# Latent attention: the probabilities' multiplication by the inverse of their sum moved from VectorE to GpSimd

## The reference

```python
def block(args):
    ql, qr = args
    s = (jnp.einsum('bqhc,bkc->bhqk', ql, c_kv)
         + jnp.einsum('bqhr,bkr->bhqk', qr, k_rope))
    p = jax.nn.softmax(s.astype(jnp.float32), axis=-1).astype(c_kv.dtype)
    return jnp.einsum('bhqk,bkc->bqhc', p, c_kv)
```

## Time and profile before

| | before |
|---|---|
| median of 3 runs | 3429.01 us (3424.55 to 3431.45) |
| the profiled execution, whole | 3426.68 us |
| its span, first to last instruction | 3425.0 us |
| PE busy | 3135.5 us, 92% |
| DVE busy | 1681.2 us, 49% |
| ACT busy | 1171.0 us, 34% |
| POOL busy | 620.6 us, 18% |
| granted TensorE clock, mean | 0.947 of full speed |

### The profile page before, as it was taken

One profiled execution on the slowest core, in us unless ns is written; L12 is line 12 of the kernel. 1 busy time (PEld: TensorE's weight loads), 2 busy tenths in 40 slices (PEclk: granted clock), 3 DMA queues, 4 the chain that ended last, 5 costly groups with the idle time before them and its releaser, 6 DMA issues.

```text
span 3425.0 us, 39752 instructions
## 1 busy us (share of the span) xinstructions
PE 3135.5 (92%) x13884; PEld 2458.6 (72%) x13884; DVE 1681.2 (49%) x2588; ACT 1171.0 (34%) x2027; POOL 620.6 (18%) x363
## 2 busy tenths in 40 slices
PE   5999969999899997588899998997999999979999
PEld 3888846888588885376588876775777767767777
DVE  5554576554553335785411113474566324745653
ACT  3222233222232323364322223534444335344442
POOL 0000000000000001001244443124211331242113
PEclk8999979999999999799899999898899998989999
DMA  4655513554343232101222332112111220121112
GB/s 187 196 176 167 176 44 123 185 176 161 115 154 117 86 110 69 28 13 35 68 87 97 98 98 75 31 56 81 56 43 44 80 74 25 56 87 56 43 39 80
DMA packets 88731, 316.03 MB, mean 92 GB/s; under 512 B 10272, under 2 KB 11168, under 8 KB 88480
## 3 DMA queue, kind: packets, MB, share of 16 engines
q1 hardware_dynamic: 65424, 235.69, 21.6%
q0 software_dynamic: 19488, 71.31, 6.2%
q10 hardware_dynamic: 3696, 7.38, 0.7%
HBM read 310.14 MB, written 2.10 MB: 91 GB/s over the span
## 4 chain that ended last, share of the span: by engine, by line
PE 43%; issue 42%; POOL 10%; DVE 3%; DMA 1%; ACT 1%; POOLq 0%; SPq 0%; DVEq 0%; ACTq 0%
PE psum L365 36%; POOL w_lo L350 10%; PE psum L1886 3%; PE psum L881 1%; PE psum L558 1%; DVE rstd L441 1%; PE psum L851 1%; DMA ada_first<-ada_in 1%; DVE ada_acc L544 1%; PE psum L1830 0%; DVE X L521 0%; DVE ta L515 0%; DVE tb L477 0%; DMA raw<-stream_in 0%; PE psum L1832 0%
## 5 line engine op out<-in xcount | busy, mean ns | idle before, releaser
L350 POOL TENSOR_TENSOR w_lo<-raw,w_hi 128x1024 fp32r<-128x1024 f32 x229 | 551.0, 2413 | 1814.8 <-ACT w_hi L321 1619.6
L365 PE MATMUL psum<-h_hi,w_hi 128*128 128x512 f32 x1856 | 501.7, 404 | 44.5 <-DVE h_lo L489 31.6
L365 PE MATMUL psum<-h_hi,w_lo 128*128 128x512 f32 x1856 | 491.9, 398 | 0.0
L365 PE MATMUL psum<-h_lo,w_hi 128*128 128x512 f32 x1856 | 491.5, 398 | 0.0
L365 PEld LDWEIGHTS psum<-h_hi,w_hi 128*128 128x128 f32 x1856 | 353.2, 191 | 138.3 <-issue 55.1
L365 PEld LDWEIGHTS psum<-h_hi,w_lo 128*128 128x128 f32 x1856 | 352.4, 190 | 85.1
L365 PEld LDWEIGHTS psum<-h_lo,w_hi 128*128 128x128 f32 x1856 | 351.9, 190 | 85.6
L335 ACT ACTIVATE w_hi<-raw 128x1024 fp32r<-128x1024 f32 x256 | 257.1, 1046 | 142.3 <-DMA raw<-stream_in 138.4
L341 DVE TENSOR_TENSOR w_lo<-raw,w_hi 128x1024 fp32r<-128x1024 f32 x192 | 227.8, 1222 | 105.1 <-ACT w_hi L335 98.5
L688 DVE TENSOR_TENSOR tb<-ta,psum 128x512 f32<-128x512 f32 x88 | 60.3, 685 | 404.0 <-PE psum L365 359.8
L642 ACT ACTIVATE a_hi<-tb 128x512 f32 (+1 forms) x88 | 55.6, 632 | 554.4 <-DVE tb L688 554.4
(11 more groups left out here) (371 smaller groups left out, 4692.0 us busy)
## 6 DMA issues: line engine op xcount, KB each, us to landing
raw<-stream_in SPq DMA_DIRECT2D x437, 512.0 KB, 3.5
ada_raw<-ada_in POOLq DMA_DIRECT2D x128, 512.0 KB, 4.6
ada_first<-ada_in POOLq DMA_DIRECT2D x2, 2048.0 KB, 21.1
ada_first<-ada_in SPq DMA_DIRECT2D x2, 2048.0 KB, 24.3
X<-xT_in ACTq DMA_DIRECT2D x1, 2048.0 KB, 8.9
out_x<-X SPq DMA_DIRECT2D x8, 256.0 KB, 2.0
qt_hi<-qr_hi ACTq DMA_DIRECT2D x16, 64.0 KB, 2.0
qt_lo<-qr_lo ACTq DMA_DIRECT2D x16, 64.0 KB, 2.0
```

The lines of the kernel that those rows point to most:

```text
L350: pool.tensor_tensor(w_lo[:, u % RING], raw[:, u % RAW], w_hi[:, u % RING].bitcast(F32), ALU.subtract).then_inc(lo_ready, 1)
L365: mm = pe.matmul(dst, w[wi], m[mi], start=(first and n == 0), stop=(last and n == total - 1), skip_group_check=skip)
```

## The change

In the latent attention alone (`by_gpsimd` true there, false in the hybrid layers), DVE makes the reciprocal, signals it on a new semaphore (`inverse_sums`) and goes on; it neither waits for the reciprocal nor multiplies. A new function `softmax_gpsimd` has GpSimd wait for the block's probabilities and its inverse sums and multiply `ta` by them in place, and give the signal on which PE's transposes wait. GpSimd's low halves of weights are written around it: the 7 units up to the output projection's first, then the 64 blocks, then the loop over the rest.

```diff
@@ split_lo_gpsimd
             pool.wait_ge(lo_ready, first)
+            for u in range(first, own["mla", "wo"]):
+                one(None, u)
+            softmax_gpsimd(pool, "mla", mla_attention)
+            first = own["mla", "wo"]
             rounds = (NU - first) // RING
@@ softmax_dve, scale(k)
                 dve.wait_ge(probs.sem, probs.at((L, k)))
                 r = small[:, 3, k % 4:k % 4 + 1]
+                if A["by_gpsimd"]:
+                    inverse.give(dve.reciprocal(r, small[:, 2, k % 4:k % 4 + 1]), (L, k))
+                    return
                 order.step(dve.reciprocal(r, small[:, 2, k % 4:k % 4 + 1]))
@@
+        def softmax_gpsimd(pool, L, A):
+
+            for k in range(4 * A["tasks"]):
+                pool.wait_ge(probs.sem, probs.at((L, k)))
+                pool.wait_ge(inverse.sem, inverse.at((L, k)))
+                p = A["p"][:, k % 2, 0:A["width"](*divmod(k, 4))]
+                probs_scaled.give(pool.tensor_scalar(p, p, small[:, 3, k % 4:k % 4 + 1], None, ALU.mult), (L, k))
+
+        inverse = Signal(sem("inverse_sums"))
@@
-            "tasks": HEADS, "width": lambda t, i: S, "scores": mla_scores,
+            "tasks": HEADS, "by_gpsimd": True, "width": lambda t, i: S, "scores": mla_scores,
```

More of the change, by code:

```diff
@@ L1084, in plan_mla @@
             plan_softmax(L, {"tasks": HEADS})
+            inverse.plan(*[(L, k) for k in range(4 * HEADS)])
             own[L, "wo"], own[L, "wog"] = cur.u, cur.g
@@ L1850, in nsa_attention @@
             return {
-                "tasks": 24, "width": lambda t, i: (i + 1) * P if t % 3 < 2 else 32, "scores": run,
+                "tasks": 24, "by_gpsimd": False, "width": lambda t, i: (i + 1) * P if t % 3 < 2 else 32, "scores": run,
                 "gate": gate, "parts": {1: (0,), 2: (1,), 3: (2,)}, "p": pn, "slots": 2,
```

## The result

The changed kernel is slower: 3443.82 us (median of 5 runs, 3443.59 to 3449.08) against 3427.32 for the kernel before (5 runs, 3424.55 to 3431.45), ratio 1.0053, 95% interval 1.0041 to 1.0066. The medians differ by 16.5 us, and the ratio makes it some 18. The time is above the upper end of the range, 3441, and it is not the forecast "no change".

The account below looks back on a forecast made before the run. DVE's throughput was taken to bound each pair's middle and latency through the multiplication its ends; seven periods at 0.00 plus 0.6 us for the last pair gave +0.6 us, forecast 3429.5 us, range 3420 to 3441.

Parts of the forecast that it names:

- no change: Whole kernel: gain mid-pair and loss at the pair's ends cancel within 7 us; 3429.5 us forecast, chance 0.59.
- d: GpSimd's multiplication of one block in the latent attention: taken as 1.0 us, with ends 0.5 and 1.5.
- The walk: Timeline of one pair of heads, 8 blocks, recomputed with GpSimd multiplying: period stays 21.10 us, block 5's transposes at 15.11.
- the second: Longer reciprocal-to-transposes way at blocks 1, 5 and 7: +14.6 us, 3444 us, if the multiplication takes 1.5; chance 0.24.
- DVE's remaining instructions are not held up beside GpSimd: DVE in the latent attention: reciprocal and `pt_lo` take as long with GpSimd working beside it; costs 0.
- The reading of 868 ns in the hybrid layers: DVE's 128x512 multiplication beside GpSimd in the hybrid layers, 868 ns against 487 with GpSimd idle, read as contention.
- The fourth rival: The bare reciprocal holds DVE as long as before, 0.19 us: +0.8 us; its chance is within the forecast's 0.59.
- the forecast 31: DVE's busy time in the latent-attention stage falls by 31 us.
- the remark that nothing but PE's work left would give 28 us: Upper limit of the gain over seven pairs, 24 plus 4 us, reaching 3401; the walk ruled it out.

## Why the prediction was wrong

**The step that failed is d**, the duration of GpSimd's multiplication: "One input is fewer here, so I take d = 1.0 us, nearer to the half of GpSimd's own row than to DVE's, and keep 0.5 and 1.5 as ends." It is 1.567, above the upper end. From 603, 924 and 1567 ns for 128, 256 and 512 columns it is 2.51 ns a column and 0.28 us fixed. The row at hand, 2413 ns for 1024 columns with two inputs, is 2.36 ns a column with the fixed part in it. Having one input fewer showed no saving. Scaled by columns that row gives 1.21 us, and 1.35 if it has a fixed part of 0.28 too (an estimate, since no run shows the subtraction's); the discount to 1.0 went the wrong way, and the measured duration is past even the end that was kept at 1.5. The Trainium skill's 769 ns for a tight loop over 512 elements, cited from "GPSIMD Engine Reference", section "Elementwise — side-by-side cycle accounting", is half of what this operation takes here.

**A second, smaller miss is in the same term.** The walk had GpSimd start 0.21 us behind the reciprocal's start (0.15, and some 0.06 for which it shows no row of GpSimd); it is 0.32. The way is 1.94 us, not the 1.27 of the forecast.

**The walk itself held.** Its own steps with 1.94 put in, counted from the transposes at 1476.26:

| step | walk | measured |
|---|---|---|
| block 1's transposes, 2.52 + 1.94 | 4.46 | 4.46 |
| `qt_lo` | 4.90 | 4.53 |
| `kt_lo`, 4.46 + 6.15 | 10.61 | 10.60 |
| block 4's reciprocal | 13.23 | 13.23 |
| block 5's transposes (one multiplication and 0.06 behind block 4's at 15.17) | 16.79 | 16.71 |
| block 7's transposes | 23.45 | 23.37 |

Seven periods of 2.35 more make 16.5, the last pair 6 blocks of (2.52 + 1.94) / 2 - 1.79 = 0.44 another 2.6: 19.1 us, against 18.5 in the stage. `qt_lo` came 0.37 earlier than in the walk, since ACT's queue began its issues at 1477.07, 0.38 ahead of the exponential; it did not matter, because `kt_hi` held `kt_lo`, as the prediction had it.

**The rivals.** The one that came true is the second, slower by a long multiplication, with 0.24; its price at d = 1.5 was 3444 us. That DVE's remaining instructions are not held up beside GpSimd was right: in the stage after, `pt_lo` took 688 ns, the maximum 683 and the reciprocal 153. The reading of 868 ns in the hybrid layers was loose: it is a mean of 24 multiplications of 0.55 us and 8 that GpSimd held, of 1.83 or 1.84. The fourth rival's worry was empty: block 1's `pt_lo` started 0.06 us behind a reciprocal. DVE's busy time fell by 26.0 us by the page, not by the forecast 31, which is what the rows of 0.49 us sum to; the multiplication took 0.40 us of DVE's time from its start to the next. Too generous was the remark that nothing but PE's work left would give 28 us: with no multiplication at all the stage gave 9.5 (some 11 by the estimate above), held there by a chain over block 6's low half that the walk did not need at d = 1.0.

**The range** was too narrow above: it stopped at d = 1.4 although the text itself kept 1.5 as an end and put the fixed part at "up to".

## What to carry to other kernels

Moving an operation off a busy engine shortens that engine's queue and lengthens the way through the operation; walk one period of the loop with both numbers, and give it only the places where the longer way is covered by other work (here 2 blocks of 8, not all, and even a third was too many). Where the second engine's price is not in the trace, scale its nearest row by columns and add a fixed part: don't discount it for a simpler operation, and let the range reach past the end that this gives. And before relieving the engine that looks full, look at what feeds it: four queue issues moved to an idle stretch gave as much as the best split did.

## What the runs showed of the hardware

- GpSimd's multiplication by a per-partition scalar, float32 in place: 603, 924 and 1567 ns for 128x128, 128x256 and 128x512, with a spread of 1564 to 1571 over 64 of the last. DVE takes 487 for the last.
- Where GpSimd is idle, it starts 0.31 to 0.35 us behind the start of the reciprocal (0.15 us long) that releases it, in every kernel here and for every width. PE starts 0.05 us behind its end.
- Two such operations in a row take 3.11 us, so the second starts 1.54 us behind the first, and at most 0.03 us of them overlap.
- A multiplication on DVE (float32, SBUF to SBUF, 128x512) that starts beside an operation on GpSimd ends 0.27 to 0.29 us behind GpSimd's, in 18 of 18 cases, so that one of 0.55 us took 1.83. `pt_lo` and the maximum, which read PSUM, and the reciprocal of one column took 688, 683 and 153 ns on average in the stage in which GpSimd multiplies, and 685, 683 and 153 in the stage in which it is idle.
- ACT's queue issues of these DMAs take 0.51 to 0.61 us, but single ones took up to 1.75 us; in one trace the three pairs with a long one were 1.6 us longer together.
